# Two decoder layers' attention regrouped: heads in pairs, three rounds a pair, transposed pieces evicted in five

## The reference, cut to what matters

```python
for l in range(DEPTH):                       # DEPTH = 2
    proj = rmsnorm_2(x, attn_norm[l]) @ w_in[l]          # sb_q, sb_k, sb_v, df_q, df_k, df_v
    # stick-breaking, 8 heads of 64
    z = q @ k.T * scale
    log_keep = where(strict, log_sigmoid(-z), 0)
    between = cumsum(log_keep, reverse=True) - log_keep
    w = where(strict, exp(log_sigmoid(z) + between), 0);  sb_out = w @ v
    # differential, 4 heads with two maps m of 64 each and values of 128
    s = q[m] @ k[m].T * scale                            # rope on q and k
    p = softmax(where(allowed, s, neg));  attn = p[0] - lam * p[1]
    df_out = rmsnorm_2(attn @ v, subln_norm[l]) * (1 - lambda_init)
    x = x + concat(sb_out, df_out) @ w_o[l]
    u = square(relu(rmsnorm_2(x, mlp_norm[l]) @ w_ff1[l]));  x = x + u @ w_ff2[l]
```

## Time and profile before

| | |
|---|---|
| median of 3 runs (range) | 1680.35 us (1679.25 to 1680.95) |
| the profiled execution: its time, its span | 1681.84 us, 1680.0 us |
| PE busy, share of the span | 1616.8 us, 96% |
| DVE, ACT, POOL busy | 935.2, 707.2, 139.1 us (56, 42, 8%) |
| granted TensorE clock, mean | 0.993 |
| chain that ended last | PE 75%, DVE 14%, ACT 5% |
| scores, L1406 | 256 matmuls |

### The profile page before, as it was taken

One profiled execution on the slowest core, in us unless ns is written; L12 is line 12 of the kernel. 1 busy time (PEld: TensorE's weight loads), 2 busy tenths in 40 slices (PEclk: granted clock), 3 DMA queues, 4 the chain that ended last, 5 costly groups with the idle time before them and its releaser, 6 DMA issues.

```text
span 1680.0 us, 20851 instructions
## 1 busy us (share of the span) xinstructions
PE 1616.8 (96%) x7745; PEld 1290.7 (77%) x7745; DVE 935.2 (56%) x1583; ACT 707.2 (42%) x1268; POOL 139.1 (8%) x131
## 2 busy tenths in 40 slices
PE   5998999999999999999999999999999999999998
PEld 4866888877778567888888888778566888888886
DVE  6566557566666765543434346566766643434343
ACT  4356532545544654422323244454664532323232
POOL 3000222031500001100000011000000200000001
PEclk8999999999999999999999999999999999999999
DMA  4211223323121101333333232211201232333331
GB/s 135 85 40 51 86 90 101 100 88 101 51 76 51 51 26 54 110 101 101 100 99 101 75 100 91 85 51 51 76 26 51 93 109 76 104 97 100 100 100 50
DMA packets 127271, 135.62 MB, mean 81 GB/s; under 512 B 2442, under 2 KB 120788, under 8 KB 127188
## 3 DMA queue, kind: packets, MB, share of 16 engines
q1 hardware_dynamic: 126084, 133.19, 24.7%
q0 software_dynamic: 288, 1.05, 0.2%
q10 hardware_dynamic: 816, 0.30, 0.1%
HBM read 132.43 MB, written 2.10 MB: 80 GB/s over the span
## 4 chain that ended last, share of the span: by engine, by line
PE 75%; DVE 14%; ACT 5%; issue 4%; DMA 1%; POOL 1%; SPq 0%; DVEq 0%; POOLq 0%; ACTq 0%
PE U L1228 21%; PE U L1230 21%; PE U L1229 21%; DVE cc L914 3%; PE Z L1406 3%; PE O L1460 2%; DVE ea L916 2%; DVE ea L911 1%; DVE pr L815 1%; PE U L1271 1%; PE U L1272 1%; PE U L1273 1%; DVE pr L833 1%; DMA raw<-in_attn_w_in 1%; PE O L1454 1%
## 5 line engine op out<-in xcount | busy, mean ns | idle before, releaser
L1228 PE MATMUL U<-XH,WL 128*128 128x512 f32 x976 | 386.3, 396 | 6.1 <-issue 5.2
L1230 PE MATMUL U<-XH,WH 128*128 128x512 f32 x976 | 381.3, 391 | 0.0
L1229 PE MATMUL U<-XL,WH 128*128 128x512 f32 x976 | 380.9, 390 | 0.0
L765 DVE TENSOR_TENSOR WL<-raw,WH 128x1024 fp32r<-128x1024 f32 x246 | 313.2, 1273 | 62.4 <-ACT WH L500 55.8
L500 ACT ACTIVATE WH<-raw 128x1024 fp32r<-128x1024 f32 x246 | 257.1, 1049 | 210.9 <-PE U L1230 173.6
L1228 PE MATMUL U<-MH,WL 128*128 128x512 f32 x848 | 335.7, 396 | 1.9 <-DVE tb L1097 1.7
L1230 PE MATMUL U<-MH,WH 128*128 128x512 f32 x848 | 330.8, 390 | 0.0
L1229 PE MATMUL U<-ML,WH 128*128 128x512 f32 x848 | 330.1, 389 | 0.0
L1228 PEld LDWEIGHTS U<-XH,WL 128*128 128x128 f32 x976 | 183.9, 188 | 44.6 <-issue 7.0
L1230 PEld LDWEIGHTS U<-XH,WH 128*128 128x128 f32 x976 | 183.7, 188 | 38.9
L1229 PEld LDWEIGHTS U<-XL,WH 128*128 128x128 f32 x976 | 184.0, 189 | 36.2
(11 more groups left out here) (219 smaller groups left out, 1756.4 us busy)
## 6 DMA issues: line engine op xcount, KB each, us to landing
raw<-in_w_ff SPq DMA_DIRECT2D x64, 1024.0 KB, 5.2
raw<-in_w_in SPq DMA_DIRECT2D x24, 1024.0 KB, 5.1
raw<-in_attn_w_in SPq DMA_DIRECT2D x10, 1024.0 KB, 5.3
raw<-in_pool_w_in SPq DMA_DIRECT2D x8, 1024.0 KB, 5.4
raw<-in_w_o SPq DMA_DIRECT2D x8, 1024.0 KB, 5.2
raw<-in_attn_w_out SPq DMA_DIRECT2D x4, 1024.0 KB, 5.0
raw<-in_pool_w_out SPq DMA_DIRECT2D x4, 1024.0 KB, 5.1
xin<-in_x SPq DMA_DIRECT2D x2, 1024.0 KB, 7.8
```

The lines of the kernel that those rows point to most:

```text
L765: v.tensor_tensor(w_slot(WL, t, shape), src, w_slot(WH, t, shape).bitcast(F32), ALU.subtract).then_inc(lo_done, 1)
L1228: mm(o, wl, xh, start=first, stop=False, **kw)
L1229: mm(o, wh, xl, start=False, stop=False, **kw)
L1230: return mm(o, wh, xh, start=False, stop=last, **kw)
```

## The change

It rewrites the attention of the two layers and leaves projections, first block and feed-forward as they are.

- **Scores in pairs.** A df head's two maps, or two sb heads, are scored together: block by block, first rows 0 to 63, then rows 64 to 127, each into a bank of its own. `Z` has 2048 columns now, `T` (one bank) stands for `PP`. A pair has three rounds (query block 3; blocks 2 and 0; block 1), alternating between the halves of `Z`, at different parts of the slots. The sb mask matmuls stand together at a round's end.
- **In place.** One buffer `W` of four rows holds exponentials, logs and weights; softplus, sum and scan overwrite it, a round of both heads in one instruction (scans by block and head).
- **Transposes** go through the one bank `T`, three times for a df head and five times for an sb pair, each evicted by one instruction (the second df one and the fourth sb one by DVE, the others by ACT).
- **Values.** For sb the outputs alternate between the partition halves of `O`, in blocks of 128 columns, in three steps a pair.
- **Order.** df head d is scored in slot 5+3d (parts 0, 1, 3), combined in the next, transposed and multiplied in slot 7+3d, squared and normed in slot 8+3d and transposed back at the head of slot 9+3d. sb pair p is scored from slot 18+2p on (positions 0, 2 and 5 in parts), transposed at 6 to 10, multiplied at 9 to 11, taken at 12.
- **GpSimd makes `WL`** for the tiles that slots 10 to 25 (layer 0) and 6 to 25 (layer 1) prepare, with the semaphore `lo_pool_done`.

```diff
+        for d in range(4):
+            first = 4 * (5 + 3 * d)
+            for i, when in enumerate((0, 1, 3)):
+                at(first + when, op="df_qk", d=d, i=i)
...
+            out_ = at(first + 11, op="df_pv", d=d)
+            at(first + 12, op="df_sq", d=d, of=out_)
+            at(first + 16, op="df_f", d=d)
...
+    POOL_LOW = {0: range(10, 26), 1: range(6, 26)}
...
+        def scores(st, head, n):
+
+            c0 = 1024 * (round_of(st) % 2) + 512 * head + (384 if n == 0 else 0)
+            return Z[:, c0:c0 + P * (n + 1)]
...
+                g.tensor_tensor(w_slot(WL, t, shape), src, w_slot(WH, t, shape).bitcast(F32), ALU.subtract).then_inc(lo_pool_done, 1)
...
+            def df_evict(st):
 
                 act.wait_ge(p0_done, st["p0"] + 1)
-                a.activation(pt[:, :, 384:512], PP[:, 0, :].rearrange("p (k q) -> p k q", q=P), ACT.Copy).then_inc(p0_free, 1)
...
+            def sb_guard(st, l):
+
+                n = 3 * (4 * l + st["p"]) + st["i"] + 1
+                dve.wait_ge(softplus_ready, n)
+                e = round_weights(st)
+                v.scalar_tensor_tensor(out=e, in0=round_scores(st), scalar=0.0, in1=e, op0=ALU.max, op1=ALU.add).then_inc(sb_guarded, 1)
...
+                for st in df_qk:
+                    df_max(st, l)
+                    if st["i"] == 0:
+                        for other in df_sq:
+                            df_mean(other, l)
...
+                for st in df_sq:
+                    df_norm(st, l)
+                if at in df_mix[l]:
+                    df_combine(df_mix[l][at], l)
...
+            def df_scores(st, l):
+
+                d, i = st["d"], st["i"]
+                pe.wait_ge(result_taken, pair_slot(l, "dfq", d)["r"] + 1)
+                pe.wait_ge(z_free, st["z"] - (1 if round_of(st) else 0))
+                for n in CHUNKS[i][2]:
+                    for m in range(2):
+                        rows_ = slice(64 * m, 64 * m + 64)
+                        last = mm(scores(st, m, n), queries[rows_, d, P * n:P * n + P], keys[rows_, d, 0:P * (n + 1)],
+                                  start=n > 0, stop=True, skip_group_check=n == 0)
+                last.then_inc(z_done, 1)
...
+                for n in CHUNKS[i][2]:
+                    for k in range(n + 1):
+                        for head in range(2):
+                            h = 2 * p + head
+                            last = mm(O[64 * head:64 * head + 64, P * n:P * n + P], values[:, k, 64 * h:64 * h + 64],
+                                      weights(pt[:, head, :], n)[:, P * k:P * k + P], start=k == 0, stop=k == n, skip_group_check=True)
```

More of the change, by code:

```diff
@@ L87, in make_plan, with at @@
             s[4]["steps"].append(use(op="stat", res=True))
-        todo = {}
+        todo = []
+        def at(position, **step):
+            todo.append((position, step))
+            return step
         for d in range(4):
[L90 to L105, removed]
+            first = 4 * (5 + 3 * d)
@@ L106, in make_plan @@
+        order = ["df_sq", "df_f", "df_t", "sb_t", "df_qk", "sb_qk", "df_pv", "sb_pv", "sb_o"]
+        for position, step in sorted(todo, key=lambda x: (x[0], order.index(x[1]["op"]))):
+            step["part"] = position % 4
+            s[position // 4]["steps"].append(use_in_place(step))
         plan["ff_stat", l] = use(op="stat")
@@ L377, in _ @@
             for src in pairs[2:]:
[L378 removed]
+                load(p, src, 2 * p - 3, p % 2)
                 p += 1
@@ L1158, in _ @@
                                 prep_lo(G_MLP + 8 * l, kt, (MH, ML))
+                    if kind == "dfk" and j == 0:
+                        dve.wait_ge(cs_landed, 16 * (l + 1))
+                    layer_slot(s, l, at, take, at not in POOL_LOW[l] and not s.get("second"))
+                    for i in range(s["n"]):
+                        take(i)
                     for st in s["steps"]:
@@ new lines, in sb_turn, with df_pv @@
+                    if i < 4:
+                        head, c0, _ = sb_t_part(i)
+                        c = c0 + P * k
+                    else:
+                        head, c = k // 2, 1024 + P * (k % 2)
+                    last = nc.tensor.transpose(T[:, P * k:P * k + P], sb_buffer(p, head)[:, c:c + P], ident[:])
+                last.then_inc(p0_done, 1)
+            def df_pv(st, l):
+                d = st["d"]
+                turned = [x for s in plan["layer", l] for x in s["steps"] if x["op"] == "df_t" and x["d"] == d][2]
+                pe.wait_ge(p0_free, turned["p0"] + 1)
+                pe.wait_ge(result_taken, pair_slot(l, "dfv", 1 + 2 * (d // 2))["r"] + 2)
+                pe.wait_ge(o_free, st["o"])
+                for n in range(NB):
+                    for k in range(n + 1):
+                        i = mm(O[:, P * n:P * n + P], weights(pt[:, d % 2, :], n)[:, P * k:P * k + P], values[:, k, P * d:P * d + P],
+                               start=k == 0, stop=k == n)
+                i.then_inc(o_done, 1)
```

677 lines of the change are left out of this document (371 added, 306 removed).

## The result

The changed kernel takes 1650.13 us (median of 4 runs, 1648.96 to 1651.60); the kernel before, on the same chip, 1679.80 us (4 runs, 1678.42 to 1680.95). Ratio 0.9827, 95% interval 0.9814 to 0.9839: faster by 1.7%. I had forecast 1641 us. The profiled executions took 1681.84 and 1651.25 us, 30.6 us apart, where my sum had 38.6.

What follows compares the result with a forecast made beforehand. PE, busy 96% of the span, bounds the kernel: stream -56.8, old waits -16.8, new waits +13.0 +8.5 +2.9 +1.1 +9.5, together -38.6 us, from 1681.8 to 1643.2 profiled, 1641 us for the median; range 1619 to 1665.

Steps and rivals of the forecast that it cites:

- Scores: PE's score groups: paired row halves overlap, fewer mode changes; df -14.2 us over eight heads, sb -28.8 us over eight pairs.
- Values: PE's sb value matmuls: both heads overlap on the array's halves, 2.8 us a pair instead of 4.5, -13.8 us.
- the other end, +4: Bound for sb values: each 128-column matmul runs alone, 5.0 us a pair, +4 us instead of -13.8.
- (a): Slots 8, 11, 14: PE waits for the df norm, now behind the third maxima; 13.0 us over both layers.
- (b): Slots 7 and 10: df transposes wait for evictions from their one bank; 8.5 us, with DVE's `WL` in layer 0.
- (c): Layer 0, slot 5: first scores wait for the residual statistic's bank, 2.9 us; slot 8 another 1.1 us.
- (d): Sb slots: late eviction at pair 0 and GpSimd holding DVE operations; 1.2 us a pair, 9.5 us over eight pairs.
- The old waits: PE's waits at sb values, df values and transposition of df outputs, 16.8 us, go; 5.8 us for the rope stays.
- The new waits: PE, now faster than the chain beside it, meets waits (a) to (d); forecast case between 20 and 50 us, 59%.
- Rival 1: ACT and DVE keep up, so (a) to (d) don't occur: 1607 us, up to 1622; 15%.
- Rival 3: Slower than before: the array's halves don't overlap in the new shapes, 1694 us; 4%.
- Rival 2: Chains longer, lateness carried into the next slot: waits double at most, 1677 us, more likely 1655 to 1662; 22%.

Runs made afterwards that it cites:

- scores_same: Changed kernel with both score matmuls of each pair taking operands from rows 0 to 63, so part of the result differs: 1674.60 us.
- values_apart: Changed kernel with only the sb value matmuls reordered, all steps of head 0 and then all of head 1: 1656.91 us.
- norm_first: Changed kernel with df_norm in front of the third round's maxima instead of behind them, nothing else: 1648.18 us.
- busy_waits: Changed kernel with 20 or 24 idle transposes of the identity in front of PE's long waits, at six places: 1645.63 us.
- later_busy: The `later` kernel with 30 to 44 transposes of the identity in front of its five remaining PE waits of 3.6 us and more: 1640.42 us.
- later: Changed kernel with norm before third maxima, layer 0's first score round one part later, df transposes, values and final part one slot later: 1640.99 us.

## Why the prediction was right or wrong

- **The number.** I said 1641 us, between 1619 and 1665; it is 1650, inside the range and faster as forecast, but 9 us slower than the forecast itself. The parts of the sum follow, with the lower clock's share taken off each and put into a term of its own.
- **Scores.** I counted -43.0 us for both kinds, transitions included. Measured: the groups alone -42.3, or -45.1 without the 2.8 us that the lower clock put into them, and 16 score groups more than before at the 0.19 us of entry and exit outside them, +3.0: -42.1. Right within 1 us. A round of 512 columns takes 1.06 us, forecast 1.2. The reason, overlap of the halves, is shown by scores_same.
- **Values.** -13.8 forecast. Measured -15.3 in the groups, with eight more of them at 0.19: -13.8. The steps stand 0.11 us apart by pairs as asked for, and values_apart shows that it is overlap. The 128-column blocks did not bring out the other end, +4.
- **(a)** 13.0 us in six entries of 1.8 or more: 12.0 us in six. Right in place and sum, though only the two of the first head are long (2.57 and 3.39), the other four are 1.5. But the cure it suggests gave 3.5 us where I expected 9 to 12: norm_first shows that the time is owed by DVE, not by the order alone.
- **(b)** four waits of 1.3 us and more, 8.5 us in all: L1605 for ACT 4.3 us in four (0.81 to 1.36), for DVE's eviction 3.7. The sum is right, its second half is not: I had 0.4 us in each of four third groups and 1.8 us for DVE's `WL`, and it came as one wait of 3.72 us in slot 7 of layer 0.
- **(c)** 2.9 and 1.1: measured 3.0 and 0.9 (L1576). Right.
- **(d)** 9.5 us over eight pairs: the mechanism is right and the place is not. DVE's scans are held while GpSimd works: timeline, changed kernel, pair 0 of layer 0 and one slot pair on:

```profile
549.30 2.41 POOL L479 TENSOR_TENSOR WL<-raw,WH 128x1024 fp32r<-128x1024 f32 x1 [8.29 <-ACT WH L582]
549.51 4.39 DVE L1060 TENSOR_TENSOR_SCAN W<-ones,W 128x512 f32<-128x512 f32 x2
...
572.23 2.34 DVE L1060 TENSOR_TENSOR_SCAN W<-ones,W 128x512 f32<-128x512 f32 x2
574.50 2.40 POOL L479 TENSOR_TENSOR WL<-raw,WH 128x1024 fp32r<-128x1024 f32 x1 [14.56 <-ACT WH L582]
```

  Two scans take 4.39 us beside GpSimd's operation and 2.34 without it. The Trainium skill, VectorE: DVE Perf Modes, section Two Vector instructions with no wait between them, speaks of a read interface shared with GpSimd, and this trace agrees, with 2.05 us for a pair. But PE waits long at pair 0 of each layer only (2.7 us twice at L1619, 2.0 twice at L1591), elsewhere 0.5 to 0.9 a time at L1619: 13.8 us with everything in it, where I had 9.5 and 20 at the upper end. How much of it is the hold isn't shown: without GpSimd's `WL` the waits at L1619 nearly went and those at L1591 stayed. That the other pairs have slack is my reading and wasn't tested.
- **The old waits.** 16.8 us were to go; they went, and 3.5 us more at the value tiles' wait for the rope (5.8 us in the earlier trace rows, 2.3 after), which I had left standing.
- **What the sum lacked** belongs to its step "**The new waits**. Here the order of the steps decides, and PE is now faster than the chain beside it": that step priced each wait at its own length and nothing behind it. The sum had no term for TensorE's clock. In the layers 20.5 us more than before run at 1.2 GHz, at half speed; 20.0 of them are not idle time, which costs 10.0 us, 4.4 inside the groups and 5.6 in the tile matmuls. With the clock's share taken off, the groups give -59.4 us (scores -45.1, values -15.3, df values -0.8, transposes +1.8). Entering and leaving more groups costs +5.9 in the tile matmuls, and with +0.1 for the statistics PE's stream is 53.3 us shorter (the parts are rounded), forecast 56.8. Waits are +15.3, forecast 18.2. With the clock's +10.0 that makes the 28.0 us by which the layers are shorter. The stream missed by 3.5 us and the waits by 2.9 the other way, which is luck; what is left of the miss is the clock. Outside the layers the profiled execution won 2.6 us, of which one slow stretch of 3.4 us less in the first block is 1.7. By the runs busy_waits takes 6.0 us back by keeping the clock up, which shows the mechanism apart from the sum.
- **Rivals.** Rival 1 (engines keep up) fell: 41.9 us of waits. Rival 3 fell with the 1.07 us rounds. Rival 2's upper path, lateness carried from slot to slot, did not come; the time lies where I had put a part of it, for another reason. The rule of the Trainium skill (TensorE: Matmul & The Clock Gate, section Measured speedup vs the span model, 3.07 for four row tiles) would have given about 1656 us, nearer than my 1641, but by a wrong cause here: two row halves run at 1.07 us against 1.93 one after the other, and the entry and exit in both, 0.2 us, leave 0.87 to 1.73, the full factor of two.

## What to carry to other kernels

A wait of the matrix engine costs its own length and perhaps clock behind it (here 1.7 us of lost work for each 3.4 us stretch): when a shorter stream runs into new waits of two to three microseconds, look at the granted clock behind each and count that time at half speed. Such a stretch costs only where PE sets the pace; where another chain does, a full clock just moves the wait. And before an instruction is moved ahead on a busy engine, ask who is late behind it: a delay of a whole slot for the consumer helped where the swap alone didn't.

## What the runs showed of the hardware that I had not expected

- Matmuls on the other half of the array overlap without strict alternation. With four of the first row half ahead nothing is lost: 1.07 us for eight in either order. With eight of the first column half ahead the overlap starts at the fifth, 1.51 us for sixteen instead of 1.02. Other numbers ahead were not tried.
- The granted clock fell for 3.4 or 6.8 us behind waits of 2.57 us and more in one profile, and in others also behind waits of 1.9 to 2.5 us. A wait's length alone doesn't decide: in `later_busy` none came behind a wait of 2.73 us (to 557.77), in the kernel before one came behind 5.8 us of values and scores of single heads, and in `scores_same`, whose score matmuls all use one row half, one lasted 17.1 us. What decides was not tested.
- Filling a wait with transposes of a constant, 0.11 us each, made neither the changed kernel nor `later` slower and kept the clock up behind most of the filled waits.
- A DVE scan of 128x384 takes 0.94 us on average where DVE makes `WL` in the sb slots, and 2.01 where GpSimd does, with its subtraction of 128x1024.
